# Projection loop of a hybrid encoder layer: decay and rate as 64-row pairs among joins and crosses, bonus, meta product and last joins moved, the rotary half turn from an SBUF copy

## What is computed

```
u = RMSNorm(h)
q, k, v, rw, gates = split(u @ w_in)              # attention q, k, v; recurrence columns; two gates
q, k = rope(q), rope(k)                           # rotary: each half times cos, other half times sin
r, k, v, xw, xa, xg = split(rw mixed with its neighbours)
decay = exp(-exp(-softplus(-(w0 + tanh(xw) @ w_up)) - 0.5))   # for both directions z = 0, 1
a     = sigmoid(a0 + xa @ a_up)                               # the rate, both directions
g     = sigmoid(xg) @ g_up
kk    = k * k_k, normalised over each head of 64
bonus = sum over a head of (r * k_dir * r_k), times v
```

## Time and profile before

| what | value |
|---|---|
| median of 3 runs | 3075.93 us |
| the profiled execution, its own time | 3075.35 us |
| its span, from first to last instruction | 3073.6 us |
| TensorE busy | 2886.7 us, 94% |
| VectorE, ScalarE, GpSimd busy | 1316.6, 981.9, 629.6 us |
| mean granted TensorE clock | 0.98 |

### The profile page before, as it was taken

How to read it: one execution, slowest core, us unless ns; L and a number is a source line. 1 busy time by engine, 2 the same in 40 slices (tenths; PEclk the granted TensorE clock), 3 DMA queues, 4 the chain that set the end, 5 groups by cost and what they waited for, 6 DMA issues and landing times. The chain is left out here.

```text
span 3073.6 us, 44642 instructions
## 1 busy us (share of the span) xinstructions
PE 2886.7 (94%) x18484; PEld 1780.3 (58%) x18484; DVE 1316.6 (43%) x2195; ACT 981.9 (32%) x1704; POOL 629.6 (20%) x370
## 2 busy tenths in 40 slices
PE   4799999999999999699999998978899999999999
PEld 3466666666666666477777877754444444444443
DVE  3375554646565554476766654545421111110100
ACT  3323232423323232455555676652200000000000
POOL 0141322313141322000000134260143323220000
PEclk9899999999999999899999999998999999999999
DMA  2142524334242524233410567854311111103100
GB/s 74 41 156 79 175 82 155 120 109 148 75 158 85 176 86 129 69 84 91 124 43 11 124 159 166 191 181 137 123 52 42 41 41 46 51 34 137 41 33 22
DMA packets 187527, 298.75 MB, mean 97 GB/s; under 512 B 84624, under 2 KB 119216, under 8 KB 180928
## 3 DMA queue, kind: packets, MB, share of 16 engines
q1 hardware_dynamic: 175232, 248.93, 27.7%
q10 hardware_dynamic: 12096, 46.99, 3.8%
HBM read 189.59 MB, written 106.27 MB: 96 GB/s over the span
## 5 line engine op out<-in xcount | busy, mean ns | idle before, releaser
L494 PE MATMUL pp_ps<-uT,pp_w 128*128 128x347 f32 x3072 | 908.8, 457 | 19.1 <-DMA pp_w<-in_w_main 19.1
L494 PEld LDWEIGHTS pp_ps<-uT,pp_w 128*128 128x128 f32 x3072 | 580.2, 190 | 334.7 <-DMA pp_w<-in_w_main 19.7
L1314 DVE TENSOR_REDUCE at_mn<-at_S 128x1 f32<-128x1040 f32 x128 | 156.0, 1239 | 51.6 <-PE at_S L1145 51.6
L1205 PE MATMUL at_ob<-at_v,at_pT 128*128 128x128 f32 (+1 forms) x1152 | 174.4, 291 | 0.0
L1145 PE MATMUL at_S<-at_kR,at_qR 64*128 64x512 f32 (+1 forms) x768 | 162.9, 501 | 10.5 <-ACT at_v L1242 5.1
L2276 PE MATMUL fd_ps<-fd_more,hidden 128*128 128x512 f32 x384 | 165.8, 592 | 0.0
L719 POOL TENSOR_TENSOR pp_neighbours<-pp_raw 128x1040 f32<-128x1040 f32 x24 | 47.8, 1994 | 566.6 <-ACT pp_raw L584 369.3
L2138 PE MATMUL fh_b<-u2T,fh_w 128*128 128x512 f32 x352 | 160.6, 599 | 2.9 <-PEq L2351 2.9
L2138 PE MATMUL fh_b<-u2T,fh_ws 128*128 128x512 f32 x352 | 158.2, 592 | 0.0
L2138 PE MATMUL fh_b<-fh_t,fh_ws 128*128 128x512 f32 x352 | 154.7, 592 | 0.0
L1205 PEld LDWEIGHTS at_ob<-at_v,at_pT 128*128 128x128 f32 (+1 forms) x1152 | 142.6, 190 | 15.4
(11 more groups left out here) (246 smaller groups left out, 4296.7 us busy)
## 6 DMA issues: line engine op xcount, KB each, us to landing
pp_w<-in_w_main SPq DMA_DIRECT2D x64, 512.0 KB, 3.7
s_kept<-pp_ob ACTq DMA_DIRECT2D x48, 520.0 KB, 4.2
fh_w<-in_w_ffn_in SPq DMA_DIRECT2D x44, 512.0 KB, 4.4
rc_kb<-s_kb SPq DMA_DIRECT2D x64, 256.0 KB, 4.1
rc_aw<-s_ar SPq DMA_DIRECT2D x64, 256.0 KB, 4.2
s_ar<-pp_ar SPq DMA_DIRECT2D x8, 1088.0 KB, 4.0
s_kb<-pp_kb SPq DMA_DIRECT2D x8, 1088.0 KB, 6.3
s_vz<-pp_vz SPq DMA_DIRECT2D x8, 1088.0 KB, 7.5
```

What stands on the lines that cost most here:

```text
L494: ins = nc.tensor.matmul(ps[s][:, n, 0:NW], weights, moving[:, n * NW:(n + 1) * NW], start=(k == 0), stop=(k == len(parts) - 1))
L1205: ins = nc.tensor.matmul(ob[:, 0:P], pT[t % 2][0:mk, b, 0:P], v[h % 2][0:mk, b, :], start=(b == 0), stop=(b == NBLK - 1))
L1314: nc.vector.tensor_reduce(mn[t % 2][:, m:m + 1], S[m][:, 0:T], AX, ALU.min).then_inc(least[m], 1)
```

## The change

- The decay and rate of one direction are made as a pair (`low_rank_pair`): a matmul with rows 0 to 63 (w) and one with rows 64 to 127 (a) alternate, each into its own slot. `pp_wl` loses its zero halves, 6 tiles to 4, and its load becomes a third smaller. The turns' order becomes w0, a0, w1, a1.
- The pairs stand between the joins and the crosses of the head before, which move up: k, joins, pair 0, crosses, pair 1, kk_sum, r. ScalarE's copies of joins and crosses move with them.
- The bonus turn moves behind att_q and grams(1). The meta product moves into att_q, behind its first third. In the last head the joins move from the place between gate_a and gate_r into gate_r, behind its second third.
- VectorE empties the first Gram halves ahead of mixing v, and the meta product behind the second terms. ScalarE raises the second logs and takes att_q ahead of bonus.
- The rotary half turn is read from `ob` in SBUF, in four passes, and the slot is free behind the first copy.

```diff
-FRONT = ["k", "w0", "w1", "a0", "a1", "kk_sum", "r", "v", "bonus", "att_q", "g", "att_k", "att_v", "gate_a", "gate_r"]
+FRONT = ["k", "w0", "a0", "w1", "a1", "kk_sum", "r", "v", "att_q", "bonus", "g", "att_k", "att_v", "gate_a", "gate_r"]
...
-        wl = sb("pp_wl", [P, 6, P])
+        wl = sb("pp_wl", [P, 4, P])
...
-                            parts = [(wl[:, 4, :], gl[:]), (wl[:, 5, :], gl2[:])]
+                            parts = [(wl[:, 2, :], gl[:]), (wl[:, 3, :], gl2[:])]
...
                         for n in range(NB):
+                            if name == "att_q" and n == 1:
+                                products(0, 0, "meta", [0])
+                            if name == "gate_r" and i == HEADS - 1 and n == 2:
+                                join_both(i)
                             for k, (weights, moving) in enumerate(parts):
                                 ins = nc.tensor.matmul(ps[s][:, n, 0:NW], weights, moving[:, n * NW:(n + 1) * NW],
                                                        start=(k == 0), stop=(k == len(parts) - 1))
                         ins.then_inc(filled[s], 1)
+
+                    def low_rank_pair(z):
+                        names = (f"w{z}", f"a{z}")
+                        for name in names:
+                            s, n_turn = slot(name, i)
+                            if n_turn >= 2:
+                                pe.wait_ge(emptied[s], n_turn - 1)
+                        for n in range(NB):
+                            for h, name in enumerate(names):
+                                s = slot(name, i)[0]
+                                ins = nc.tensor.matmul(ps[s][:, n, 0:NW], wl[half[h], z, :],
+                                                       lor[half[h], n * NW:(n + 1) * NW], start=True, stop=True)
+                                if n == NB - 1:
+                                    ins.then_inc(filled[s], 1)
...
                     turn_of("k")
                     pe.wait_ge(wl_here, 16 * i + 16)
-                    for name in ("w0", "w1", "a0", "a1", "kk_sum"):
-                        turn_of(name)
                     if i >= 1:
                         join_both(i - 1)
-                    turn_of("r")
+                    low_rank_pair(0)
                     if i >= 1:
                         for b in range(2):
                             cross(b, i - 1)
+                    low_rank_pair(1)
+                    turn_of("kk_sum")
+                    turn_of("r")
                     turn_of("v")
                     grams(0)
-                    turn_of("bonus")
-                    products(0, 0, "meta", [0])
                     turn_of("att_q")
                     grams(1)
+                    turn_of("bonus")
                     for name in ("g", "att_k", "att_v", "gate_a"):
                         turn_of(name)
-                    if i == HEADS - 1:
-                        join_both(i)
                     turn_of("gate_r")
...
-                        nc.scalar.activation(banked(ob[n % 2][:]), cols(ps[s]), ACT.Copy, scale=scale)
+                        nc.scalar.activation(banked(ob[n % 2][:]), cols(ps[s]), ACT.Copy, scale=scale).then_inc(emptied[s], 1)
+                        act.wait_ge(emptied[s], slot(name, i)[1])
                         if (name, i) != ("att_q", 0):
                             act.wait_ge(rope_summed, 2 * i + (name == "att_k"))
                         for q in range(4):
-                            ins = nc.scalar.activation(half_turned[quarter[q ^ 1], 0:NW * 2].rearrange("p (n w) -> p n w", n=2),
-                                                       ps[s][quarter[q], 0:2, 0:NW], ACT.Copy, scale=scale)
-                            ins = nc.scalar.activation(half_turned[quarter[q ^ 1], NW * 2:T], ps[s][quarter[q], 2, 0:T - 2 * NW],
-                                                       ACT.Copy, scale=scale)
-                        ins.then_inc(emptied[s], 1)
+                            ins = nc.scalar.copy(half_turned[quarter[q ^ 1], :], ob[n % 2][quarter[q], 0:T])
+                        ins.then_inc(halves_swapped, 1)
...
+                    if i >= 1:
+                        keep_join(i - 1)
                     squash(0, "w0")
-                    squash(1, "w1")
+                    squash(2, "a0")
...
-                    squash(2, "a0")
+                    squash(1, "w1")
                     squash(3, "a1")
                     s, n_turn = slot("kk_sum", i)
                     act.wait_ge(emptied[s], n_turn)
                     nc.scalar.activation(raw[:, 1:T + 1], raw[:, 1:T + 1], ACT.Sqrt).then_inc(once["kk_root"], 1)
                     raise_logs(0)
                     if i >= 1:
-                        keep_join(i - 1)
+                        keep_cross(i - 1)
                     take_mixed("r")
-                    if i >= 1:
-                        keep_cross(i - 1)
                     take_mixed("v")
+                    raise_logs(1)
+                    keep_for_rope("att_q", 0)
                     s = fill("bonus")
                     act.wait_ge(bonus_stored, 16 * i + 16)
                     nc.scalar.copy(banked(bv[:]), cols(ps[s])).then_inc(emptied[s], 1)
-                    raise_logs(1)
-                    keep_for_rope("att_q", 0)
                     keep_turn("g", 1)
...
-                            pool.wait_ge(gram_filled[b], gram_count(i, b, "meta" if b == 0 else "z0") if z else
+                            pool.wait_ge(gram_filled[b], gram_count(i, b, "z0") if z else
...
-                        s, n_turn = slot(name, i)
                         at = 2 * i + (name == "att_k")
-                        pool.wait_ge(emptied[s], n_turn)
+                        pool.wait_ge(halves_swapped, at + 1)
...
-                    dve.wait_ge(vz_stored, 16 * i + 16)
-                    mix("v", vz[:, :, CH:P])
                     dve.wait_ge(x_stored, 16 * i + 16)
                     keep_gram(0, "z0", slice(0, 8))
                     keep_gram(1, "z0", slice(8, 16))
+                    dve.wait_ge(vz_stored, 16 * i + 16)
+                    mix("v", vz[:, :, CH:P])
+                    shrink_terms(1)
                     keep_gram(0, "meta", slice(NU, NU + 1))
-                    shrink_terms(1)
+                    keep_gram(1, "z1", slice(24, 32))
+                    keep_gram(0, "z1", slice(16, 24))
                     read("bonus")
                     after(dve, "mixed_v", i)
                     nc.vector.tensor_tensor(by_step(bv[:, META:T]), by_step(bv[:, META:T]), vz[:, 1:NS, CH:P],
                                             ALU.mult).then_inc(once["bonus_done"], 1)
-                    keep_gram(1, "z1", slice(24, 32))
-                    keep_gram(0, "z1", slice(16, 24))
...
-        w_low[:, N:, 2 + z] = a_up[z].transpose(1, 0, 2)
-    w_low[:, :, 4] = g_up[:P].transpose(1, 0, 2)
-    w_low[:, :GL - P, 5] = g_up[P:].transpose(1, 0, 2)
+        w_low[:, N:, z] = a_up[z].transpose(1, 0, 2)
+    w_low[:, :, 2] = g_up[:P].transpose(1, 0, 2)
+    w_low[:, :GL - P, 3] = g_up[P:].transpose(1, 0, 2)
```

7 lines of the change are left out of this document (3 added, 4 removed).

## The result

The changed kernel takes 3046.11 us (median of 4 runs, 3041.96 to 3050.11) against 3077.55 us for the one before on the same chip (4 runs, 3075.9 to 3081.36). The ratio after to before is 0.9902, with a 95% interval of [0.9887, 0.9918]: 31.4 us faster, where 38.9 were forecast (3037 us against 3075.93). The profiled execution of after was its slowest, 3050.11 us; that of before took 3075.35 us.

What follows compares the result with a forecast made beforehand. The projection loop was taken as a TensorE stream with some 23 us of holes, ScalarE setting the new stretch. Terms -21.8 + 1.1 - 11.9 - 5.9 = -38.5 from 3075.35 gave 3037 us; range 3029 to 3056, the case's own 3029 to 3045.

Steps and rivals of the forecast that it cites:

- a wait of grams(1): Rival: second terms come too late and grams(1) waits for VectorE's meta copy; 3045 to 3053 us, chance 0.13.
- its own signs: Trace checks: no last-join wait, clock 1.00 through gate_r, heads 4.6 us shorter; wrong if the clock falls inside the loop.
- Part 1: Decay and rate pairs among joins and crosses: a pair takes 1.9 us, 3.1 us gained a head, -21.8 us over seven.
- The loss of 30%: Skill-page estimate for the 64-row pairs: imperfect row packing would make a pair 2.4 us; the prediction took 1.9.
- Head 0: First head, with no joins to fill with: r starts at 11.75 us instead of 10.63, +1.1 us.
- Part 2: Meta product inside att_q, bonus behind it: need 2.0 us instead of 3.48, 1.5 us a head, -11.9 us.
- Part 4: VectorE's chain behind w1 runs 4.4 us later; slack before grams(1) shrinks from 10 us to about 2, costed at nothing.
- Part 3: Last head's join moved into gate_r: its 2.93 us wait and the half-clock losses behind it go, -5.9 us.
- SP's queue holds the second store, vz and the att_v weights: Transfers behind the later meta copy: claimed free, because att_v is wanted over 25 us later.
- worth nothing: Early release of att_q's slot by the half turn: no gain, since no TensorE wait went to the half turn.
- serial pairs: Rival: the 64-row matmuls of a pair don't overlap, so their saving doesn't exist; 3064 us, chance 0.05.
- The clock's rival: Rival: TensorE's clock falls in the new stretch; once per head 3061 us, chance 0.05; twice 3091, chance 0.04.

Runs made afterwards that it cites:

- full-row turns: The changed kernel with the four low-rank turns as full 128-row matmuls on zero-padded weights, one after the other, in the same places: 3063.44 us, ratio 0.9965 to before.
- old places, filled: The changed kernel with pairs kept, joins and crosses in their former places, useless products ahead of each pair and kk_sum in every head: 3069.37 us, ratio 0.9975.
- stores last: The changed kernel with SP sending and reloading all blocks, then loading att_v weights, before storing second terms, ge and vz: 3044.99 us, ratio 0.9894 to before.

## Why the prediction was right, and where not

- **The number.** 3046.1 us lies in the stated range, but by luck: the forecast's own range was 3029 to 3045, and what widened it, a wait of grams(1) priced at 3045 to 3053, didn't occur. The time got there by a step that stood in no rival, the last head. By its own signs the prediction was wrong in that place: the last join waits, and the clock falls inside the loop.
- **Pairs (Part 1): right.** A pair takes 2.02 us (1.95 start to start), k to r 12.07 us for 11.85: 2.9 us a head instead of 3.1, together -20.2 for -21.8. Most of the difference is pair 1, which begins at 7.0 us and not at 6.67, with a wait of 0.39 for ScalarE's tanh. The loss of 30% that the prediction estimated from the Trainium skill (TensorE: Matmul & The Clock Gate, "Part 3: Packing small matmuls") was not to be seen: 2.02 us against 1.92 for six full-row instructions. Head 0: 11.68 us, +1.05 for +1.1.
- **Where that gain comes from:** less from the overlap (undone alone, 1.56 us a head: full-row turns) than from the joins and crosses that fill the time in which ScalarE empties k and the first pair (undone alone, up to 4.6 us a head with the clock held up, the useless products' own time included: old places, filled). The two can't be added: together they exceed the 2.9 us. Full-row turns in the old places, with the rest of the change kept, were not run. And the gain comes only with Part 2: alone it leaves 0.5 us a head.
- **Bonus and meta (Part 2): right in size, wrong in rank.** The meta product stands in att_q at 0.26 us (451.35 to 451.61) without a wait and bonus takes 1.86 (463.15 to 465.01), so 2.1 for 3.5: about 1.4 us a head, -11.2 for -11.9. But undone alone, it costs 3.9 us a head (138.3 for 134.36). Part 4 put VectorE's lateness at nothing; it costs nothing because Part 2 covers it.
- **The lateness (Part 4): right for VectorE.** The first terms' last store (s_kb) was issued 43.4 us after k (447.66 - 404.29; forecast 43.0), the meta copy ended at 55.2 (forecast 55.8), and grams(1) came at 56.9 without a wait. Timeline of VectorE, head 2:

```profile
455.01 1.23 DVE L811 TENSOR_TENSOR pp_kb<-pp_th,pp_shrink 128x1024 f32<-128x1024 f32 x1 [3.30 <-DMA s_kb<-pp_kb]
456.15 3.19 DVE L813 TENSOR_TENSOR pp_kb<-pp_th,pp_shrink 128x1024 f32<-128x1024 f32 x1
459.27 0.21 DVE L819 TENSOR_TENSOR pp_xa<-pp_gram,pp_mask 128x64 f32<-128x64 f32 x1
```

- **The last head (Part 3): the step that failed.** "Two thirds into gate_r, 9.5 us later, the blocks have been there for over 6 us" was wrong twice. TensorE's way from k to gate_r became some 4.6 us shorter, a figure that the prediction has among its signs and that Part 3 leaves out. That alone leaves 2 of the 6.6 us: the join's place is 110.9 + 9.5 - 4.6, or 115.7 us after k as measured with the stores last, and before, the blocks were there at 113.8. And the blocks came 5.5 us later, at 119.3, through "SP's queue holds the second store, vz and the att_v weights ..., so this is free": I had asked who needs att_v and not who needs the blocks in the same queue. The meta copy's new place has 2.6 us of that lateness at the inversion; the rest came with the second blocks right behind the stores. From gate_a's end to the crosses 0.45 us were lost instead of 5.9 saved: 6.3 us of the sum. Stores last put it right: no wait, and no fall of the clock in gate_r.
- **The half turn:** "worth nothing" holds for before only; in the new order it is 1.7 us a head. It cost the sum nothing, since the change includes it. The copies from SBUF took 1.06 us each, as estimated.
- **The sum:** -20.2 + 1.05 - 11.2 + 0.45, and 0.8 for the two waits for weights, give -29.1; the loop shows -29.3. Of the 9.2 us that it falls short of -38.5, 6.3 are the last head, 2.3 the smaller gains of Parts 1 and 2 and 0.8 the weights (0.2 too many in all). The median's miss is as large, 3046.1 for 3037.
- **The rivals.** Neither grams(1)'s wait nor serial pairs occurred. The clock's rival did not in this kernel's profile, but close to it: with the pairs in the old places, waits of 2.3 us before each were enough in seven heads of eight, and the result is slower than before.

## What to carry over

When a stretch of one engine is shortened, lay out the chains of the other engines again from the new zero: slack that was read in the old trace shrinks by what was saved, and a move that is free for its own data can delay another's in the same queue. A small load that starts a long chain goes ahead of the large stores, and so do its own small stores; moving only one of the two moves the delay. What lies between two short pieces of matmul work is worth as much as the pieces: here the filler (joins and crosses) brought more than the overlap. Where the clock fell in seven heads, even useless products beat idle time; in head 0 alone their gain was not seen in the medians.

## What the hardware showed unexpectedly

- Two 64-row matmuls in different row halves overlap almost completely, weight loads included: 12 instructions over 347 columns in 2.02 us, against 1.92 for 6 with full rows, and 3.75 for 12.
- The granted clock fell to 0.50 (1.2 instead of 2.4 GHz) in stretches in which TensorE worked 2 us and waited 2.3 us, several times in a row, and this cost 3.5 us a head beyond the waits (24.3 over the seven heads in which it fell). With bonus and meta back ahead of att_q, waits of 1.9 us did it in heads 1 to 3 for 6.8 us each, and in the later ones for 3.4 us or not at all. The waits of after from head 1 on, 0.2, 0.4 and 1.2 us, did not do it. In head 0 of the new order, with waits of 2.3, 2.3 and 1.2 us, it fell in some executions and not in others.
- Four transfers of blocks cost SP 1.97 us to issue when no transfer was under way, and 5.76 us behind five large ones. A load of blocks that was issued behind the stores was used 12.5 us later, one ahead of them 3.9 us later (63.1 to 67.0 after k).
